# A two-block transformer kernel: the opening norm moved around the modulation, head norms taken by tokens, reordered mixer ends, a later wait for the second weight slot

## What is computed

```
# first block, layer l (x: 512 tokens, ctx: 256 tokens)
m = silu(c) @ ada_w[l] + ada_b[l]                        # six vectors of 1024
h  = rms_norm(x, norm_mix[l])   * (1 + sc_m)  + sh_m      # ctx: the same with its own csc_m, csh_m
# layer 0 (even mixer): differential attention, 4 heads of 128, beside a gated delta rule
o = softmax(q1 k1^T) v - lam * softmax(q2 k2^T) v         # per head, [tokens, 128]
a = rms_norm(o, subln) * (1 - lam_init)                   # norm of every token over the head's 128
out = concat(a, b) @ w_out
# layer 1 (odd mixer): neighbourhood attention with a table of relative biases (rpb)
# second block: forgetting attention (log_sigmoid gates, cumulative sum) beside retention,
#   whose output is centred, normed per head and multiplied by silu(rg); then @ w_out
```

## Time and profile before

| | us |
|---|---|
| median of 3 runs | 3742.7 (3740.07 to 3755.59) |
| the profiled execution | 3749.85 |
| its span, first to last instruction | 3748.1 |
| PE busy / DVE / ACT / POOL | 93% / 40% / 34% / 31% of the span |
| mean granted TensorE clock | 0.970 of full speed |

### The profile page before, as it was taken

The page is one execution under the profiler, slowest core; times in us unless marked ns, Lnnn a source line. Parts: engine busy times, 40 slices in busy tenths (PEclk is TensorE's granted clock), DMA queues, the critical chain, the costliest instruction groups (busy, mean ns, idle before and its releaser), DMA issues.

```text
span 3748.1 us, 60177 instructions
## 1 busy us (share of the span) xinstructions
PE 3503.5 (93%) x24152; PEld 3031.3 (81%) x24152; DVE 1510.3 (40%) x2656; ACT 1269.5 (34%) x1808; POOL 1171.1 (31%) x812
## 2 busy tenths in 40 slices
PE   6998878888999999999999999998999999989998
PEld 4677667877788788888778888978999988777887
DVE  4976754434121222565532124454312244542121
ACT  3545432223111111355544223254432232544222
POOL 1221112213222233121145453223444532234453
PEclk9999889989999999899999999999999999999999
DMA  4310000001432311111123232111222211122222
GB/s 193 130 68 29 31 1 2 2 13 63 174 125 84 142 64 65 35 40 46 41 79 105 88 104 66 57 46 63 78 96 84 95 67 58 46 68 87 98 95 90
DMA packets 65310, 273.56 MB, mean 73 GB/s; under 512 B 9841, under 2 KB 10993, under 8 KB 62065
## 3 DMA queue, kind: packets, MB, share of 16 engines
q1 hardware_dynamic: 61120, 268.04, 20.8%
q10 hardware_dynamic: 4016, 3.03, 0.3%
HBM read 268.95 MB, written 2.10 MB: 72 GB/s over the span
## 4 chain that ended last, share of the span: by engine, by line
issue 52%; PE 20%; POOL 19%; DVE 6%; ACT 1%; DMA 1%; POOLq 0%; SPq 0%; ACTq 0%; DVEq 0%
POOL w_lo L370 18%; PE ps L382 9%; PE ps L1052 3%; DVE arena L1343 2%; DVE arena L1329 1%; DMA raw<-in_even_in 1%; PE ps L1548 1%; PE ps L1137 1%; PE ps L1554 0%; PE ps L1115 0%; DVE arena L1350 0%; PE ps L1457 0%; PE ps L1125 0%; PE ps L1128 0%; POOLq L365 0%
## 5 line engine op out<-in xcount | busy, mean ns | idle before, releaser
L370 POOL TENSOR_TENSOR w_lo<-raw,w_hi 128x512 fp32r<-128x512 f32 (+1 forms) x760 | 1098.6, 1467 | 2296.0 <-ACT w_hi L315 2296.0
L315 ACT CAST w_hi<-raw 128x1024 fp32r<-128x1024 f32 (+1 forms) x380 | 419.7, 1104 | 1486.7 <-PE ps L382 1176.1
L382 PE MATMUL ps<-act_hi,w_hi 128*128 128x512 f32 (+2 forms) x2304 | 655.8, 339 | 19.1 <-POOL w_lo L370 13.6
L382 PE MATMUL ps<-act_lo,w_hi 128*128 128x512 f32 (+2 forms) x2304 | 651.7, 337 | 0.0
L382 PE MATMUL ps<-act_hi,w_lo 128*128 128x512 f32 (+2 forms) x2304 | 651.4, 337 | 0.0
L382 PEld LDWEIGHTS ps<-act_hi,w_hi 128*128 128x128 f32 x2304 | 406.6, 189 | 82.6 <-issue 22.6
L382 PEld LDWEIGHTS ps<-act_hi,w_lo 128*128 128x128 f32 x2304 | 408.7, 189 | 48.0
L382 PEld LDWEIGHTS ps<-act_lo,w_hi 128*128 128x128 f32 x2304 | 408.9, 189 | 45.9
L514 DVE TENSOR_TENSOR nscr<-nscr,ps 128x512 f32<-128x512 f32 (+2 forms) x132 | 69.7, 556 | 851.4 <-PE ps L382 829.0
L382 PE MATMUL ps<-ff_hi,w_hi 128*128 128x512 f32 (+2 forms) x1056 | 297.0, 335 | 0.0
L382 PE MATMUL ps<-ff_hi,w_lo 128*128 128x512 f32 (+2 forms) x1056 | 297.0, 335 | 0.0
(11 more groups left out here) (420 smaller groups left out, 5587.6 us busy)
## 6 DMA issues: line engine op xcount, KB each, us to landing
raw<-in_gu SPq DMA_DIRECT2D x176, 512.0 KB, 3.3
arena<-in_ada SPq DMA_DIRECT2D x24, 2048.0 KB, 8.1
raw<-in_dn SPq DMA_DIRECT2D x64, 704.0 KB, 4.0
raw<-in_in SPq DMA_DIRECT2D x56, 512.0 KB, 3.3
raw<-in_even_in SPq DMA_DIRECT2D x28, 512.0 KB, 3.4
raw<-in_odd_in SPq DMA_DIRECT2D x24, 512.0 KB, 3.3
raw<-in_out SPq DMA_DIRECT2D x16, 512.0 KB, 3.3
raw<-in_even_out SPq DMA_DIRECT2D x8, 512.0 KB, 3.3
```

The lines of the kernel that those rows point to most:

```text
L315: act.copy(w_hi[:, j, 0:cols], raw[:, j, 0:cols]).then_inc(s["hi_ready"], 1)
L370: ins = pool.tensor_tensor(w_lo[:, j, c], raw[:, j, c], w_hi[:, j, c].bitcast(F32), ALU.subtract)
L382: mm = pe.matmul(ps[:, 2 * j + b, 0:cn], wt[:, j, w], acts[:, k, c0:c0 + cn], start=(k == 0 and wt is w_hi and acts is hi), stop=(k == kt ...
```

## The change

Five things are edited. (1) The opening norm goes by tokens like the later ones, in a stage `open` that also holds the modulation: PE does chunk 0, sums, chunk 1, spread, then the rest; DVE adds up squares and then multiplies x by the row into free rows of the arena; ACT squares, roots, copies the four chunks and splits the weights last. `dve_norm(first)` becomes one `tensor_scalar` (times amod, plus shift) on each piece, ACT copies, DVE subtracts. (2) The differential output is weighed with operands swapped, so a tile has tokens on partitions; each unit's squares are summed by ACT (`accum_out`), the root and reciprocal are of 128x6, one multiply scales the head, PE transposes it back, DVE multiplies by `subln`. (3) In the odd mixer, bias tables 0 and 1 go between the fresh steps. (4) In the second block's mixer `log_forget` and `scan_forget` move two places back, `take` goes ahead of `finish_group`, and parts 0 and 1 go ahead of the split. (5) Fresh output projections wait for slot 0 alone and go four k on slot 0, four on slot 1, then the rest; slot 1 is waited for at its first use.

```diff
-        def pe_products_fresh(pe, halves, fresh, begun=0):
+        def pe_products_fresh(pe, halves, fresh, begun=0, late=None):
             order = [(k, j) for k in range(KD // 2) for j in range(SLOTS)] + [(k, j) for j in range(SLOTS) for k in range(KD // 2, KD)]
+            if late is not None:
+                order = [(k, j) for half in (range(KD // 2), range(KD // 2, KD)) for j in range(SLOTS) for k in half]
             if begun:
                 order = [(k, j) for j in range(SLOTS) for k in range(0 if j else begun, KD)]
             for k, j in order:
                 if j == 0:
                     pe.wait_ge(s["parts_ready"], fresh + k + 1)
+                elif k == 0 and late is not None:
+                    pe.wait_ge(s["lo_ready"], late)
                 w = slice(k * P, (k + 1) * P)
                 for wt, acts in ((w_hi, act_hi), (w_hi, act_lo), (w_lo, act_hi)):
                     for b, (c0, cn) in enumerate(halves):
...
             if fresh is not None:
-                pe.wait_ge(s["lo_ready"], b0 + SLOTS)
+                pe.wait_ge(s["lo_ready"], b0 + 1)
                 pe.wait_ge(s["tile_read"], read0 + SLOTS)
-                pe_products_fresh(pe, halves, fresh, n.pop("begun"))
+                pe_products_fresh(pe, halves, fresh, n.pop("begun"), b0 + SLOTS)
...
-                if a is None:
+                if a is None or shift == 0:
                     ins = act.copy(act_hi[:, k, c0:end], y[:, c0:end])
...
-                if a is None:
+                if a is None or first:
...
+                elif first:
+                    for h0, hn in halves:
+                        z = 1 if h0 == 0 else 0
+                        ins = dve.tensor_scalar(y[:, h0:h0 + hn], open_rows(k)[:, h0:h0 + hn], amod[:, a, k, z:z + 1], mod[:, shift + k, z:z + 1],
+                                                ALU.mult, ALU.add)
...
+        def open_rows(k):
+            return nscr[:, 2, 0:T] if k == KD - 1 else arena[:, A_SIZE - (k + 1) * T:A_SIZE - k * T]
+
+        def pe_open(pe, n):
+            chunks = norm_chunks(BOTH)
+
+            def products(r):
+                pe.wait_ge(ada_landed[r], 16)
+                pe_ada_products(pe, ada_ring[:, r, :], 2 + r % 2)
+
+            def turn(r):
+                pe.wait_ge(s["ada_rows"], r + 1)
+                pe_ada_turn(pe, ada_front[:, r, :], 6, 8 * r)
+
             pe.wait_ge(s["act_chain"], 1)
             pe.wait_ge(s["ada_blank"], 1)
-            for r in range(4):
-                pe.wait_ge(ada_landed[r], 16)
-                pe_ada_products(pe, ada_ring[:, r, :], 2 + r)
-                if r:
-                    pe.wait_ge(s["ada_rows"], r)
-                    pe_ada_turn(pe, ada_front[:, r - 1, :], 6, 8 * (r - 1))
-            pe.wait_ge(s["ada_rows"], 4)
-            pe_ada_turn(pe, ada_front[:, 3, :], 6, 24)
-
-        def act_ada(act, n):
+            products(0)
+            pe.wait_ge(s["squares_added"], KD - 1)
+            for i, (c, _) in enumerate(chunks):
+                pe.matmul(ps[:, 7, 2 * i:2 * i + 2], nscr[:, 3, c:c + P], ones[:, 0:2], start=True, stop=True)
+            pe.wait_ge(s["squares_ready"], KD)
+            for i, (c, _) in enumerate(chunks):
+                mm = pe.matmul(ps[:, 7, 16 + 2 * i:18 + 2 * i], nscr[:, 1, c:c + P], ones[:, 0:2], start=True, stop=True)
+            mm.then_inc(s["norm_sums"], 1)
+            products(1)
+            pe.wait_ge(s["norm_scale"], 1)
+            for i, (c, cn) in enumerate(chunks):
+                mm = pe.matmul(norm_row[:, P * i:P * i + cn], norm_scales[:, 2 * i:2 * i + 1].to_broadcast([P, P]), ident[:, P - cn:P],
+                               start=True, stop=True)
+            mm.then_inc(s["norm_rows"], 1)
+            turn(0)
+            products(2)
+            turn(1)
+            products(3)
+            turn(2)
+            turn(3)
+
+        def act_open(act, n):
+            for k in range(KD):
+                if k >= 2:
+                    act.wait_ge(s["squares_added"], k - 1)
+                act.activation(nscr[:, k % 2, 0:T], x[:, k, :], ACT.Square).then_inc(s["squares_ready"], 1)
+            act_norm_rows(act, n, BOTH)
             for r in range(4):
                 act.wait_ge(s["ada_used"], r + 1)
-                act.copy(ada_front[:, r, :], ps[:, 2 + r, :]).then_inc(s["ada_rows"], 1)
+                act.copy(ada_front[:, r, :], ps[:, 2 + r % 2, :]).then_inc(s["ada_rows"], 1)
+            for j in range(SLOTS):
+                act_split(act, j, 16, FULL)
+
+        def dve_open(dve, n):
+            total = nscr[:, 3, 0:T]
+            dve_link(dve, n, dve.memset(total, 0.0))
+            for k in range(KD - 1):
+                dve.wait_ge(s["squares_ready"], k + 1)
+                if k:
+                    dve.wait_ge(s["squares_added"], k)
+                dve.tensor_tensor(total, total, nscr[:, k % 2, 0:T], ALU.add).then_inc(s["squares_added"], 1)
+            dve_norm_rows(dve, n, BOTH)
+            for k in range(KD):
+                ins = dve.tensor_tensor(open_rows(k), x[:, k, :], norm_row[:, 0:T], ALU.mult)
+            dve_link(dve, n, ins)
 
...
+                if kind == "sub":
+                    pe.wait_ge(s["diff_scaled"], i // 2 + 1)
+                    c0, cn = BOTH[i % 2]
+                    for t in range(cn // P):
+                        mm = pe.transpose(ps[:, 7, t * P:(t + 1) * P], dq[:, i // 2, c0 + t * P:c0 + (t + 1) * P], ident)
                     mm.then_inc(s["front_post"], 1)
                     return
...
-                    mm = pe.matmul(ps[:, 6, 2 * P:3 * P], dv[e % 2][:, j, :], dpt[:, u % 2, j * P:(j + 1) * P],
+                    mm = pe.matmul(ps[:, 6, 2 * P:3 * P], dpt[:, u % 2, j * P:(j + 1) * P], dv[e % 2][:, j, :],
...
+            def square_out(u, at):
+                e, t, _ = diff_unit(u)
+                act.wait_ge(s["diff_taken"], u + 1)
+                if u:
+                    act.wait_ge(s["diff_squared"], u)
+                act.activation(fsq[:, 1 if at % 6 < 3 else 0, 0:P], dq[:, e, t * P:(t + 1) * P], ACT.Square, accum_out=out_sums(e)[:, t:t + 1]
+                               ).then_inc(s["diff_squared"], 1)
+                if u % 6 == 5:
+                    act.wait_ge(s["diff_squared"], u + 1)
+                    act.activation(out_sums(e), out_sums(e), ACT.Sqrt, bias=eps_ap, scale=1.0 / P).then_inc(s["diff_root"], 1)
...
+                    if u >= 2:
+                        square_out(u - 2, at)
...
+            def scale_out(e):
+                dve.wait_ge(s["diff_root"], e + 1)
+                dve_link(dve, n, dve.reciprocal(out_sums(e), out_sums(e)))
+                y = dq[:, e].rearrange("p (t f) -> p t f", f=P)
+                dve.tensor_tensor(y, y, out_sums(e).unsqueeze(2).to_broadcast([P, NCH, P]), ALU.mult).then_inc(s["diff_scaled"], 1)
+
+            def finish_out(i):
+                c0, cn = BOTH[i % 2]
+                dve.wait_ge(s["front_post"], front_no["sub", i] + 1)
+                dve.tensor_scalar(dq[:, i // 2, c0:c0 + cn], ps[:, 7, 0:cn], v("subln"), None, ALU.mult).then_inc(s["front_post_read"], 1)
...
+                if at in (39, 45, 51):
+                    scale_out((at - 39) // 6)
...
+                        if k in (3, 5):
+                            bias((k - 3) // 2)
...
+                    if at == ITEMS2 - 1:
+                        act.wait_ge(s["fox_taken"], u0 + UNITS2)
+                        part(0)
+                        part(1)
                     split(at // 2)
-                if at == 2:
-                    log_forget()
...
+                if at == 2:
+                    log_forget()
...
-                if at == 3:
+                if at == 5:
...
                 if u is not None and u < UNITS2:
                     normalise(u)
+                if u:
+                    take(u - 1)
                 for e in (first, then):
                     if e and e[0] == "square":
                         finish_group(e[1])
-                if u:
-                    take(u - 1)
                 if at % 2 == 0 and 2 <= at <= 16:
```

104 lines of the change are left out of this document (28 added, 76 removed).

## The result

The changed kernel took 3724.23 us (median of 6 runs, 3721.7 to 3728.01) beside 3741.74 for the kernel before in the same session: 17.5 us less; the ratio of the runs, which isn't that of the two medians, is 0.9943 with a 95% interval of 0.993 to 0.9956. In a second session the unedited changed kernel gave 3722.32 beside 3746.01 (0.9933, 0.9919 to 0.9946), 23.7 less. So the gain is 17 to 24 us, where 27 was forecast. The profiled execution: 3728.01 us, span 3726.2, against 3749.85 and 3748.1.

The account below looks back on a forecast made before the run. PE, busy 3503.5 of 3748.1 us, bounds the kernel; only its idle time and lower-clock work can be won. Terms -7-8.5-1.5-3.2-4.6-2.2 = -27 gave 3722.9 beside the profiled execution, 3716 as median; range 3703 to 3731.

Parts of the forecast that it names:

- opening: Start of the front: first parts at 49.8 instead of 53.95, then seven shorter steps; -7 us, bounds -2 and -11.
- head norm, body: Attention units: PE's 4.36 us wait at item 46 shrinks, less ACT's new squares (-1.9), and a shorter half-clock spell (-0.6).
- head norm, tail: Last `take` to the end of the head norm, nothing hiding it: 12.0 us becomes 6.0, so -6.0.
- odd mixer: Two of four bias tables fill PE's waits between the fresh steps: -1.75, +0.2 for what doesn't fit; -1.5 (0 to -2).
- log_forget, twice: Second block: the swap no longer stands behind table loads, so PE's 1.6 us eviction wait goes; -1.6 each, -3.2.
- take, twice: Second block: `take` ahead of `finish_group` saves 1.4 of wait, the half-clock spell behind it goes too; -2.3 each, -4.6.
- projection, twice: Fresh output projection: PE starts about 2.1 us earlier, then waits again for parts 2 and 3; -1.1 each, -2.2.
- the one for an earlier item 0: Opening: the front's first parts come at 49.8 us, y of step 0 at 45.5; -4.1 us.
- 4 to 5 us of work at half speed add 2 to 2.5: Opening: allowance for PE's queue at 0.50 clock after idling from about 22 to 28.6; at worst all 14.3 doubles.
- The sentence that gave -4 by the Trainium skill's rule: Opening: if DVE and POOL exclude each other, POOL's work costs the steps up to 5 us, not 1.7; opening then -4.
- moved waits only move: Rival: only tail and opening arrive, -13, and `scale_out` stalls the third and later heads by 2; 3732 us, chance 0.04.
- The slower rival (ACT as the bound): Attention units: ACT's added square and accumulator read, 0.6 us per unit, lie on the path; +24, 3767 us, chance 0.04.

Follow-up runs that it names:

- the undone trace: Changed kernel with edits 4 and 5 put back as before (second block's mixer order, fresh output projections): 3728.63 us, ratio 0.9949 to the kernel before.
- the second pair: Changed kernel and kernel before, each run once more with nothing edited, for a second trace: 3722.32 us and 3744.57 us.
- The undone parts: Changed kernel with one piece put back per run: opening 3723.79 us, head norm 3734.45, bias tables 3733.26, edits 4 and 5 together 3728.63.

## Why the prediction was right or wrong

The time (3724.2, or 3722.3) lies in the range, and every part gained. Whether it passed the prediction's line of 0.5% (3724) is close: by the ratio it did (0.57%, interval 0.44 to 0.70, and 0.67% in the second session), by the first session's medians just not (0.47%). The sum was too large: by the stage table, means of two traces,

| term | forecast | measured |
|---|---|---|
| opening | -7 | -4.0 |
| head norm, body | -2.5 | -2.3 |
| head norm, tail | -6.0 | -5.1, and +1.2 behind it |
| odd mixer | -1.5 | -2.7 |
| log_forget, twice | -3.2 | -3.7 |
| take, twice | -4.6 | -1.9 |
| projection, twice | -2.2 | -2.1 (with the undone trace among the old ones) |

which adds up to 20.6, between the two measured gains. The misses partly cancel: the opening, the take and the tail gave 3.0, 2.7 and 2.1 us less than forecast, the odd mixer and `log_forget` 1.2 and 0.5 more. That the time lies in the range owes something to that.

**Opening.** Of its two terms, the one for an earlier item 0 (-4.1) failed and the one for shorter steps (-3.1) held (3.3, and 1.77 us a step against 1.8). Item 0 came 1.1 us earlier against the first trace of before and 1.7 later in the second pair. The step that failed is "4 to 5 us of work at half speed add 2 to 2.5". Work that is priced at full rate adds its whole length at half rate: the sums and chunk 1, priced 2.8 and 1.8, cost 5.4 and 3.2, so they added 4.0. The full price itself was right (twelve records took 1.50 at full clock, where 1.4 was put). The second step is POOL beside the y's, charged 1.7 and measured 4.44-1.65 = 2.8. And the base of 53.98 was the slow end: the old opening came at 52.15 and 52.19 in its other traces. The sentence that gave -4 by the Trainium skill's rule (SBUF — State Buffer, Who interferes with whom) named the right amount for the part by luck: it put up to 5 us on POOL, which cost 2.8 of its 5.16, and says nothing of the sums on PE.

**Head norm.** Body and mechanism were right, item 46 to the tenth (2.09, "about 2"). In the tail the small terms were low: the two groups of transposes took 0.66 and 1.12 at 0.50 of the clock, where 0.35 and 0.6 had been put. The price of what follows wasn't in the sum: the even mixer pays 1.2, in a longer half-clock stretch 289 us behind the gates. There the traces with the new and the old tail still stand level.

**Odd mixer.** Mis-sized downwards: the prediction counted only PE's idle time between the steps. In this stage it fell from 2.2 and 3.0 us in the two traces of before to 1.2 and 1.3; the rest of the gain is fewer or shorter half-clock stretches, which the sum left out.

**Take.** The step "the half-clock spell behind it goes as well" failed in its worth. The spell did go, in all 22 passes, but PE then waited 1.5 us for `normalise` in the same item, a wait that the sum didn't have. Like for like a pass gains 1.6 to 1.7, not 2.3. This is the rival "moved waits only move", in one place.

**Projection.** Size and form came as forecast ("a second, new one for the third part"), but the first pass gives anything from +0.4 to -2.5 by pairs of traces, and the second wait was put down to gates that wait for ACT, while the rows show DVE's gate products beside POOL. The slower rival (ACT as the bound) is out: ACT is busy 8.3 us less than before, and PE's waits for its copies show no new row in the body. (That rival's own sum had a slip: the other parts without the body are 24.5, not 19, so it stood at 3761.)

**What stays open**: why the kernel with the old opening isn't slower as a whole, beyond that its even mixer had fewer half-clock stretches, and what decides where a half-clock stretch falls. The undone parts add up to 0.2+10.9+9.7+5.1 = 25.9 us, more than the whole change; the parts needn't be independent, since an edit can move the half-clock stretches of the code behind it, but with about 5 us of uncertainty on each ratio the excess isn't told from noise either.

## What to carry to other kernels

Price PE work that may fall into a half-clock stretch at twice its full-rate price, not at half as much again; and when a wait is removed, ask what PE, now earlier, will wait for next, before the half-clock stretch behind it is counted as gained. A window that reads full clock ahead of a trace's first clock entry says nothing: read the records' durations there. For edits worth a few us, compare stages between the same records over two or three traces of each kernel: here that resolves 0.1 us where waits decide and 1.5 to 5 where the clock does (the even mixer took 343.2 to 348.9 us with the same code), while the gain in medians moved by 6 us between two sessions. Where a DVE operation from SBUF to SBUF meets POOL's work, put there one that isn't needed next, or move POOL's work under operations that read PSUM.

## What the runs showed of the hardware

Three things weren't expected. First, PE can run at half rate for long at the start of a program. In the 14 traces the first clock entry, a rise to full clock, stands between 23.1 and 39.4 us, 3 to 20 us behind the first of the opening's PE work. With the new opening, chunk 0 took 3.4 to 3.6 us for 16 records that take 1.90 at full clock, and after 5.3 to 5.5 us of idle the twelve sum records took 2.72 us in all seven unedited traces.

Second, moving two tables of biases changed PE's busy time by 11 us, with the same 24164 records, through where the half-clock stretches fell.

Third, DVE operations met POOL's weight splits with very different results. Four `tensor_scalar` pieces from SBUF to SBUF took 4.44 us beside them and 1.65 alone, two products of two SBUF operands 2.77 and 0.77, and seven multiplies with one operand in PSUM 6.14 both ways.

The windows for the changed kernel show how long a half-clock stretch can be where PE is busy only part of the time: the tail and the gates, and a later stretch of the even mixer.
```profile
484.00:501.00 17.00, 9.89 (x43) 9.03 (x44) 8.26 (x10) 6.99 (x10) 1.90 (x1) 0.50 0.00 1
777.50:784.50 7.00, 5.68 (x28) 5.39 (x27) 5.02 (x7) 2.03 (x3) 0.00 (x0) 0.51 0.00 0
```
In the kernel before the clock over the same records (789.16 to 796.16, 5.68 us busy as well) is 0.80. That second stretch, 6.8 us at half clock with the new tail and 3.4 with the old one, is where the 1.2 us behind the tail went.
